# A hybrid block on Trainium2: fillers in quarters, and new orders around RWKV, keys and sums

## What is computed

```python
h = (_rms(x, norm1_g[l]) * valid).astype(dt)
z = h @ w_in[l]
aq, ak, av, bq, bk, bv, bg, c_in, dq, dk, dv, gz = _split(z, IN_SIZES)
y_sb = stick_breaking_attention(...)       # 8 heads of 64
y_ret = silu(bg) * retention(...)          # 4 heads, 64 keys, 128 values
y_rw = rwkv7_mix(...)                      # 8 heads of 64, normalised by head, bonus, gate
y_sw = sliding_window_attention(...)       # 8 query heads, 2 key heads, window 128
merged = (gates[:, :, 0] * (y_sb @ p_sb[l]) + gates[:, :, 1] * (y_ret @ p_ret[l])
          + gates[:, :, 2] * (y_rw @ p_rw[l]) + gates[:, :, 3] * (y_sw @ p_sw[l]))
x = x + merged @ w_o[l]
x = x + squared_relu_mlp(_rms(x, norm2_g[l]), w_up[l], w_down[l])
```

## Time and profile before

| | |
|---|---|
| median of 3 runs | 1204.14 us (1203.28 to 1204.44) |
| time of the profiled execution | 1203.32 us |
| its span in the trace | 1201.6 us |
| TensorE busy | 1175.7 us (98%) |
| VectorE, ScalarE, GpSimd busy | 502.9, 489.8, 468.5 us |
| share of TensorE in the chain that ended last | 82% |

### The profile page before, as it was taken

The page is one execution under the profiler, slowest core; times in us unless marked ns, Lnnn a source line. Parts: engine busy times, 40 slices in busy tenths (PEclk is TensorE's granted clock), DMA queues, the critical chain, the costliest instruction groups (busy, mean ns, idle before and its releaser), DMA issues.

```text
span 1201.6 us, 20666 instructions
## 1 busy us (share of the span) xinstructions
PE 1175.7 (98%) x8782; PEld 962.4 (80%) x8782; DVE 502.9 (42%) x994; ACT 489.8 (41%) x808; POOL 468.5 (39%) x288
## 2 busy tenths in 40 slices
PE   8999999999999899999999999999999999999998
PEld 7998877887788578667777787778888888888887
DVE  4799435454554553533362585272522000222000
ACT  6455323222323443776635634443643312243210
POOL 3443435325443125323342532353334544344541
PEclk9999999999999999999999999999999999999999
DMA  6222323222222142211522221242232323232330
GB/s 250 89 73 86 116 80 107 65 76 96 89 73 72 35 146 65 65 36 71 197 88 62 86 76 53 73 174 88 70 105 88 123 92 102 70 106 88 123 123 35
DMA packets 35998, 111.47 MB, mean 93 GB/s; under 512 B 4273, under 2 KB 9137, under 8 KB 35394
## 3 DMA queue, kind: packets, MB, share of 16 engines
q1 hardware_dynamic: 30288, 98.59, 24.5%
q10 hardware_dynamic: 5106, 11.43, 2.7%
q0 software_dynamic: 512, 0.13, 0.1%
HBM read 99.43 MB, written 9.04 MB: 90 GB/s over the span
## 4 chain that ended last, share of the span: by engine, by line
PE 82%; DVE 10%; ACT 5%; POOL 2%; issue 2%; DMA 0%; DVEq 0%; ACTq 0%
PE pst L1843 18%; PE pst L1845 17%; PE pst L1844 17%; PE pst L2019 5%; PE pst L2017 5%; PE pst L2018 5%; POOL w_lo L814 1%; PE pst L2358 1%; ACT w_hi L932 1%; PE pst L2350 1%; PE pst L2136 1%; PE pst L2083 1%; PE pst L2320 1%; PE pst L2335 1%; DVE cdif L1411 1%
## 5 line engine op out<-in xcount | busy, mean ns | idle before, releaser
L814 POOL TENSOR_TENSOR w_lo<-raw,w_hi 128x1024 fp32r<-128x1024 f32 x164 | 402.3, 2458 | 634.0 <-ACT w_hi L932 622.3
L1843 PE MATMUL pst<-h_hi,w_hi 128*128 128x512 f32 (+1 forms) x704 | 255.5, 363 | 1.3 <-DVE h_lo L1384 0.7
L1845 PE MATMUL pst<-h_hi,w_lo 128*128 128x512 f32 (+1 forms) x704 | 242.8, 345 | 0.0
L1844 PE MATMUL pst<-h_lo,w_hi 128*128 128x512 f32 (+1 forms) x704 | 242.5, 344 | 0.0
L932 ACT ACTIVATE w_hi<-raw 128x1024 fp32r<-128x1024 f32 x164 | 171.9, 1052 | 140.2 <-PE pst L2019 114.2
L1843 PEld LDWEIGHTS pst<-h_hi,w_hi 128*128 128x128 f32 x704 | 133.1, 189 | 25.4 <-issue 5.7
L1845 PEld LDWEIGHTS pst<-h_hi,w_lo 128*128 128x128 f32 x704 | 132.9, 189 | 15.9
L1844 PEld LDWEIGHTS pst<-h_lo,w_hi 128*128 128x128 f32 x704 | 133.2, 189 | 15.1 <-issue 2.2
L1843 PE MATMUL pst<-x_hi,w_hi 128*128 128x512 f32 (+1 forms) x272 | 102.6, 377 | 0.4 <-DVE x_lo L1715 0.4
L1844 PE MATMUL pst<-x_lo,w_hi 128*128 128x512 f32 (+1 forms) x272 | 102.4, 377 | 0.0
L1845 PE MATMUL pst<-x_hi,w_lo 128*128 128x512 f32 (+1 forms) x272 | 102.4, 376 | 0.0
(11 more groups left out here) (339 smaller groups left out, 2022.7 us busy)
## 6 DMA issues: line engine op xcount, KB each, us to landing
raw<-in_weights SPq DMA_DIRECT2D x164, 512.0 KB, 3.3
xt<-in_x SPq DMA_DIRECT2D x4, 512.0 KB, 5.0
wait_gate<-stage ACTq DMA_DIRECT2D x8, 256.0 KB, 2.7
gate_t<-wait_gate ACTq DMA_DIRECT2D x1, 2048.0 KB, 9.4
x<-in_x ACTq DMA_DIRECT2D x1, 2048.0 KB, 7.9
out<-x SPq DMA_DIRECT2D x7, 256.0 KB, 3.6
cst<-in_consts SPq DMA_DIRECT2D x1, 1524.0 KB, 10.7
wait_ret_g<-stage ACTq DMA_DIRECT2D x4, 256.0 KB, 3.0
```

Of the source, the lines that this page charges most:

```text
L814: nc.gpsimd.tensor_tensor(w_lo[:, u % W_SLOTS, :], raw[:, u % RAW_SLOTS, :], w_hi[:, u % W_SLOTS, :].bitcast(F32), ALU.subtract).then_inc( ...
L1843: M(out, lh, rh, start=(first and i == 0), stop=False)
L1844: M(out, lh, rl, start=False, stop=False)
L1845: last = M(out, ll, rh, start=False, stop=(final and i == len(terms) - 1))
```

## The change

It has five parts. (1) In RWKV blocks 1 to 4 the piece between the two groups of state products moves to the block's very end, behind the outputs (`after`); in block 0 it moves behind the second group. (2) In the normalisation the next tile's sum and bonus are issued without waiting for the previous tile's finished value; only the gate product waits, and half of the tile's pieces stand in front of it; VectorE's low part of tile t comes behind the centring of tile t+2, and `POST_SUM`, `POST_BONUS`, `POST_GATE` count the products in their new order. (3) `sb_keys` moves behind the first two value jobs. (4) In `sb_arg` the first product of the low carries, which lets ScalarE begin, comes ahead of the four own products of the low parts. (5) `gate` jobs are cut into four pieces instead of two and `proj` jobs into two instead of one, and the lists are doubled; in stick-breaking five quarters instead of four stand in front of the sums of heads 1, 3 and 5, and one quarter each is taken away before retention, behind its last norm and at the window's end. All other counts are the old ones, doubled. In the window, two pieces move between the first and the second score products.

```diff
@@ -41,16 +41,16 @@
...
-RW_FILL = [dict(tok=1, score=0, c1=[3, 1, 1, 1, 1], tu=[0, 1, 1, 2, 2], f=1, wz=1, mn=1, end=2)] + \
-          [dict(tok=1, score=0, c1=[3, 1, 1, 1, 1, 1], tu=[0, 2, 2, 2, 2, 2], f=1, wz=1, mn=1, end=3)] * NB
+RW_FILL = [dict(tok=1, score=0, c1=[3, 1, 1, 1, 1], tu=[0, 1, 1, 2, 2], f=1, wz=1, mn=0, end=3, after=0)] + \
+          [dict(tok=1, score=0, c1=[3, 1, 1, 1, 1, 1], tu=[0, 2, 2, 2, 2, 2], f=1, wz=1, mn=0, end=3, after=1)] * NB
...
-SB_FILL = [(2, 0)] * 7 + [(2, 2)]
+SB_FILL = [(4, 0), (5, 0)] * 3 + [(4, 0), (4, 4)]
...
-RET_FILL = [(2, 1)] * 5
-RET_POST_FILL = [(0, 1), (1, 2), (1, 2), (2, 2)]
-SW_FILL = [(2, 2)] + [(1, 2)] * 6 + [(1, 1)]
-SW_END_FILL = 2
+RET_FILL = [(4, 2)] * 5
+RET_POST_FILL = [(0, 2), (2, 4), (2, 4), (4, 3)]
+SW_FILL = [(4, 4)] + [(2, 4)] * 6 + [(2, 2)]
+SW_END_FILL = 3
@@ -139,7 +139,7 @@
...
-PARTS = {**dict.fromkeys(("aq", "ak", "bq", "bk", "bg", "dq", "dk", "rgate"), 4), "bv": 2, "bdv": 3, "gate": 2}
+PARTS = {**dict.fromkeys(("aq", "ak", "bq", "bk", "bg", "dq", "dk", "rgate"), 4), "bv": 2, "bdv": 3, "gate": 4, "proj": 2}
@@ -579,6 +579,8 @@
...
+
+        POST_SUM, POST_BONUS, POST_GATE = [1, 3, 6, 9], [2, 5, 8, 11], [4, 7, 10, 12]
@@ -625,9 +627,9 @@
...
             g("sb_prep")
-            g("sb_keys")
             g("sb_z", 0)
             jobs(2)
+            g("sb_keys")
             g("sb_soft", 0)
             jobs(NB - 2)
@@ -650,7 +652,7 @@
...
             g("ret_prep")
-            pieces(2)
+            pieces(3)
             g("ret_gate")
@@ -678,9 +680,11 @@
...
             for i in range(2 * NB):
+                if i == 0:
+                    pieces(2)
                 if i + 1 < 2 * NB:
                     g("sw_scores", i + 1)
-                pieces(SW_FILL[i][0])
+                pieces(SW_FILL[i][0] - (2 if i == 0 else 0))
                 g("sw_turn", i)
@@ -1800,28 +1807,34 @@
...
             def post_center(t):
-                dve.wait_ge(post_done, 3 * t + 1)
+                dve.wait_ge(post_done, POST_SUM[t])
...
+            def post_low(t):
+                dve.wait_ge(yh_ready, t + 1)
+                if t == 0:
+                    for i in range(2):
+                        dve.wait_ge(spill_out[i], 16 * ((len(SPILL_NO) + 1 - i) // 2))
+                V.tensor_tensor(y_lo[:, t, :], KR[:, t, 0, MB:L], y_hi[:, t, :].bitcast(F32), ALU.subtract)\
+                    .then_inc(yl_ready, 1)
 
             post_center(0)
             for t in range(4):
                 y = KR[:, t, 0, MB:L]
-                dve.wait_ge(post_done, 3 * t + 2)
+                dve.wait_ge(post_done, POST_BONUS[t])
                 V.tensor_tensor(post["bon"][:], pst[:, 5, :], RV[:, t, MB:L], ALU.mult)
                 if t < 3:
                     post_center(t + 1)
+                if t:
+                    post_low(t - 1)
                 dve.wait_ge(postr_ready, t + 1)
                 link(V.tensor_tensor(y, y, post["rs"][:], ALU.mult))
                 link(V.tensor_scalar(y, y, PAR("rw_ln_g", t), PAR("rw_ln_b", t), ALU.mult, ALU.add))
                 link(V.tensor_tensor(y, y, post["bon"][:], ALU.add))
-                dve.wait_ge(post_done, 3 * t + 3)
+                dve.wait_ge(post_done, POST_GATE[t])
                 V.tensor_tensor(y, y, pst[:, 6, :], ALU.mult).then_inc(yf_ready, 1)
-                dve.wait_ge(yh_ready, t + 1)
...
+            post_low(3)
@@ -1970,12 +1983,17 @@
...
                 elif kind == "proj":
-                    s = job_begin(n)
-                    pe.wait_ge(yl_ready, y_count(a) + 4)
+                    s = job_slot(n)
+                    if part == 0:
+                        job_begin(n)
+                        pe.wait_ge(yl_ready, y_count(a) + 4)
                     us = u % W_SLOTS
                     ws = [slice(2 * P * k + P * (b % 2), 2 * P * k + P * (b % 2) + P) for k in range(4)]
-                    product3(pst[:, 2 * s, :], [((w_hi[:, us, ws[k]], w_lo[:, us, ws[k]]), (y_hi[:, k, :], y_lo[:, k, :]))
-                                                for k in range(4)]).then_inc(dense_done, 1)
+                    last = product3(pst[:, 2 * s, :],
+                                    [((w_hi[:, us, ws[k]], w_lo[:, us, ws[k]]), (y_hi[:, k, :], y_lo[:, k, :]))
+                                     for k in range(2 * part, 2 * part + 2)], part == 0, part == 1)
+                    if part == 1:
+                        last.then_inc(dense_done, 1)
@@ -2111,10 +2129,10 @@
                 pe.wait_ge(cs_split, 2 * h + 1)
                 add(0, P, ones, sb_cs_hi[:, 0:SBW[1]])
                 add(1, P, ones, sb_cs_hi[:, SBW[1]:])
+                pe.wait_ge(cs_split, 2 * h + 2)
+                add(0, P, ones, sb_cs_lo[:, 0:SBW[1]]).then_inc(z_arg, 1)
                 pe.wait_ge(s_lo, 2 * h + 2)
                 add_own(1, 1)
-                pe.wait_ge(cs_split, 2 * h + 2)
-                add(0, P, ones, sb_cs_lo[:, 0:SBW[1]]).then_inc(z_arg, 1)
                 add(1, P, ones, sb_cs_lo[:, SBW[1]:]).then_inc(z_arg, 1)
                 for cs in (sb_cs_hi, sb_cs_lo):
                     last = add_meta(P, cs[:, 0:SBW[1]])
@@ -2437,6 +2455,7 @@
...
                     last.then_inc(yy_done, 1)
+                pieces(fill["after"])
@@ -2444,17 +2463,29 @@
...
-            post_sum(0)
-            for t in range(4):
+            def post_bonus(t):
+                M(pst[:, 5, :], headsum, BON[:, t, MB:L], start=True, stop=True).then_inc(post_done, 1)
+
+            def post_gate(t):
                 if t:
                     pe.wait_ge(yf_ready, t)
-                M(pst[:, 5, :], headsum, BON[:, t, MB:L], start=True, stop=True).then_inc(post_done, 1)
                 M(pst[:, 6, :], g2[:, P * t:P * t + P], SG[:, MB:L], start=True, stop=True).then_inc(post_done, 1)
+
+            post_sum(0)
+            post_bonus(0)
+            post_sum(1)
+            post_gate(0)
+            for t in range(4):
                 pe.wait_ge(postq_ready, t + 1)
                 M(pst[:, 7 - 4 * (t % 2), :], headsum, post["sq"][:], start=True, stop=True).then_inc(postv_done, 1)
-                if t < 3:
-                    post_sum(t + 1)
-                pieces(RW_NORM_FILL[t])
+                if t:
+                    post_bonus(t)
+                    if t < 3:
+                        post_sum(t + 1)
+                pieces(RW_NORM_FILL[t] // 2)
+                if t:
+                    post_gate(t)
+                pieces(RW_NORM_FILL[t] - RW_NORM_FILL[t] // 2)
```

More of the change, by code:

```diff
@@ L904, in _ @@
                     pieces(fill["c1"][l] + fill["tu"][l])
-                pieces(fill["f"] + fill["wz"] + fill["mn"] + fill["end"])
+                pieces(fill["f"] + fill["wz"] + fill["mn"] + fill["end"] + fill["after"])
             pieces(sum(RW_NORM_FILL))
@@ L1348, in _ @@
                 act.wait_ge(postv_done, t + 1)
+                if t:
+                    act.wait_ge(yf_ready, t)
                 link(A(post["rs"][:], pst[:, 7 - 4 * (t % 2), :], ACT.Ln, scale=1.0 / HD, bias=RW_LN_EPS))
@@ L1817, in _ @@
                 link(V.tensor_tensor(y, y, post["bon"][:], ALU.add))
-                dve.wait_ge(post_done, 3 * t + 3)
+                dve.wait_ge(post_done, POST_GATE[t])
                 V.tensor_tensor(y, y, pst[:, 6, :], ALU.mult).then_inc(yf_ready, 1)
-                dve.wait_ge(yh_ready, t + 1)
-                if t == 0:
-                    for i in range(2):
-                        dve.wait_ge(spill_out[i], 16 * ((len(SPILL_NO) + 1 - i) // 2))
-                V.tensor_tensor(y_lo[:, t, :], y, y_hi[:, t, :].bitcast(F32), ALU.subtract).then_inc(yl_ready, 1)
+            post_low(3)
             run_after_rw(pieces, jobs, dict(
```

## The result

The changed kernel takes 1220.35 us (median of 4, 1215.69 to 1222.02), the kernel before on the same chip 1203.84. The ratio is 1.0131, 95% interval 1.0102 to 1.0159: slower, as forecast, but 10 us more than the 1210.5 of the prediction and outside its range of 1203.5 to 1214.0. The profiled execution is the quickest of the four, 1215.69.

A forecast was written before the change was run, and what follows sets the result against it. TensorE bounds the kernel, busy 1175.7 of 1201.6 us. Gains -8.5, stick-breaking +5.9, retention +3.7, later tanh +0.5, window +4.8 make +6.4; 1203.32 + 6.4 + 0.8 = 1210.5 us, range 1203.5 to 1214.

The forecast's parts named there:

- I add 0.15 a wait: Waits of TensorE: each costs 0.15 us beyond its idle row, as one row showing 0.31 lost 0.46.
- Stick-breaking: Heads 1, 2, 3 wait for late merges to free banks, losing 2.4, 2.1, 3.7 us; net 5.9 slower, bounds 4 and 7.
- head 5: Stick-breaking: the chain through ScalarE, VectorE and GpSimd outlasts TensorE's work, so the fifth quarter is hidden, 1.4 us.
- Retention: Last gate's tanh runs ahead of the first key norm, so TensorE waits for scaled keys: 3.7 us, bounds 2 and 5.4.
- The later tanh: Tanh of the retention gates stands ahead of a square and a norm: 0.5 us charged, bounds 0 and 2.
- Rival 4: Key norm, last retention norm: two-input VectorE instructions meeting weight subtractions take 1.76 more each, +3.5 us: 1214.0; chance 0.1.
- The window: Sliding window: first three turns wait for merges, 6.7 us in all, less 1.9 gained; 4.8 slower, bounds 0 and 8.
- The gains: RWKV ends 3.6, normalisation 3.1, keys' copies 1.8 us: together 8.5 us faster.
- Rival 1: Late merges hit stick-breaking but only one later stage: 1206.3 us without retention's loss, 1203.8 without the window's; chance 0.18.
- rival 2: Banks are free in time in retention and window; only stick-breaking loses: -4.5, 1199.6 us; chance 0.08.
- rival 3: No bank is waited for at all, in any stage: -15.9, 1188.2 us; chance 0.04.

The follow-up runs named there:

- the third bank: Changed kernel with a third PSUM bank for projections 67 and 70, so jobs 67 to 71 wait for the job three before: 1201.37 us, ratio 0.9982.
- the aligned kernel: All five parts of the change on the kernel before, but every list of piece counts simply doubled: 1193.36 us, ratio 0.9908.
- the window and retention experiments: Against the aligned kernel: only the window's groups a quarter off, 1200.01 us, ratio 0.9965; only retention's pieces two quarters ahead, 1199.91 us, ratio 0.9969.
- the experiment with the fives alone: The aligned kernel with five quarters in heads 1, 3 and 5, and one instead of four before retention: 1211.41 us, ratio 1.0059.

## Why the prediction was wrong

**The price of a wait.** The step that failed is in the prediction's second paragraph: "A wait costs more than its idle row" and "I add 0.15 a wait." The clock is in no term of the sum; it was put at nothing without a reason. I had read the clock column of the kernel before, 1.00 in every stretch, as a property of the kernel. It went with its waits, none of which was longer than 1.6 us from the first products on, and not even so in every execution. Nor does the column tell all: in the same trace, products of 272 columns start 0.23 us apart until about 17 us (14.17, 14.40) and 0.13 apart from there on (17.64, 17.77), which is half speed at the program's start under a column of 1.00. The new waits of 2.6 to 4.9 us cost 5.7 us of clock in the profiled execution; with spare products in them the median is 8.3 us lower. With the four longest waits filled the forecast holds: 1212.1 measured, 1210.5 predicted. From what the runs show now, the clock should stand as a term of 0 to 2 us behind each of the seven new waits, 0 to 14 in all, and the range would reach above 1220.

**The load before retention.** The change takes a piece away there; I followed what the shift does to the tanh and the merges, not that this stretch also covers a load issued at its start. Cost 1.4, shown by two doses (3.9 us of waiting at one quarter, 1.3 at three, none at four and six).

**Stick-breaking** was right term by term, +5.9 against +5.9 without the clock, and its cause is shown by the third bank, which returns the three heads to 11.7, 12.7 and 11.8 us. That the order of the sums helps only where the chain leaves slack was right for head 5 by the same reason; for odd heads with four quarters I first expected a gain in the aligned kernel and there was none.

**Retention** was right in mechanism and within 0.4 in size (4.1 against 3.7; VectorE's 1.72 instead of 1.10 is that difference and more). The later tanh cost nothing. Rival 4 priced a meeting with a weight subtraction at a fixed 1.76 us; it is what is left of the subtraction, 0.6 more here than before.

**The window** came out as 6.7 for its three waits, as predicted, though by turn it is 2.2 three times and not 2.0, 2.4 and 2.4. Done alone it costs 6.65 too; that the two agree is luck, as 1.7 of it is clock, and two other waits, 1.6 and 0.8, are spared. It depends on a single quarter: all pieces are whole jobs again in the aligned kernel, and the waits vanish.

**The gains** were 9 to 9.6 instead of 8.5. Rival 1 and rival 2 fall with the window and retention experiments, rival 3 with the traces. Rival 4 came true in the changed kernel only with the 0.6 us of the key norm, but in full when a quarter more was moved.

Open: why the clock falls behind one wait and not behind another, longer one, in the same execution (head 1 at 3.5 us no, head 2 at 2.6 yes; head 1 yes in the experiment with the fives alone). The runs show that it varies between executions, not what decides. The three executions of the changed kernel around its median have no trace, so their further 4 to 6 us are laid to the clock by its mean alone. I also did not separate the RWKV ends from the normalisation on the chip; the traces alone give the two together as -7.6. Nor did I try VectorE's merges ahead of the sums, which would free the banks without a third one.

## What to carry to other kernels

Cut filler jobs as finely as you like, but see where each stretch of filler begins and ends: with two banks, and an engine that empties them only between its own steps, a stretch of four quarters may open two jobs when it starts on a job's boundary, and must not open a third. Count a wait of TensorE of some microseconds twice, once for itself and once, from nothing to 2.3 us here, for the clock behind it; where it can't be removed, cheap products into a free bank buy the second part back. When a count of pieces changes, list what its stretch covers besides the thing in view: loads issued at its start, table changes behind a job's end, subtractions on GpSimd.

## What the runs showed of the hardware that was not expected

- TensorE's granted clock fell to 0.50 for about 3.4 us behind idle times of 1.3 us (once), 2.0, 2.6 and 4.9 us, and for 6.8 us around one of 4.1; behind one of 3.5 it stayed at 1.00 in one execution and fell in another kernel's. Executions of one kernel differ by this: 1215.7 us at a mean clock of 0.994, 1222.0 at 0.987.
- A VectorE instruction with two SBUF inputs of 128x4 elements, usually 0.16 to 0.23 us, took 1.66 beside a 128x1024 subtraction on GpSimd, and ended with it. The collision costs what is left of the other engine's instruction, whatever one's own size.
- At the program's start products of 272 columns run at half speed, 0.23 us from start to start instead of 0.13, under a clock column of 1.00. This ended near 16.2 us in the profiled execution with retention's pieces ahead and near 18.7 in the aligned one, and head 0's scores then start 1.2 us apart (420.45 and 421.64): executions of otherwise like work differ by this before anything of the change has run.
